# Projections of a hybrid decoder step: the sample rows' column-group steps in pairs behind every second place

## The chip, the cores and the metric

One core of one Trainium2 chip runs the whole kernel. The metric is the device time of one execution in microseconds (us), from its runs the median.

## The reference, cut to what matters

The reference is one inference step of two decoder layers for a prompt group (1024 rows) and a sample group (8 sequences of 4 new rows, 32 rows together) that share the same weights. Three things in it are large matrix products of rows with a weight matrix, and the change is in these alone:

```
layer 0:  h0 = rmsnorm(x) @ even_w_in      rows x 1024 by 1024 x 3584
          x1 = x + (mix0 * silu(z)) @ even_w_out      1024 x 1024
layer 1:  h1 = rmsnorm(x1) @ odd_w_in                 1024 x 2864
          x2 = x1 + (mix1 * silu(z)) @ odd_w_out      1024 x 1024
          y  = rmsnorm(x2)
```

Between them stand the attention and retention parts of the two layers. Each product is wanted for the 1024 prompt rows and for the 32 sample rows. The change alters no value that is computed and no sum's order.

## The kernel before, in words

**Tiling of the prompt rows.** The contraction of 1024 is cut into KD = 8 slices of 128. The prompt rows are NT = 8 tiles of 128 rows. The weight columns are cut into chunks that fit one accumulator bank of 512 columns: 7 chunks of 512 in the first projection, 3 chunks of 342 or 340 for an output projection, 6 chunks of 478 (the last 474) for the second input projection. One row tile against one column chunk is called a *place* here, and places are numbered through a projection (chunk times 8 plus tile). A place is 24 matmuls into one bank: for each slice three products of split operands (`y_lo` with `w_hi`, `y_hi` with `w_lo`, `y_hi` with `w_hi`). These are L489 (`h_acc`) in `project` and L1115 (`x_acc`) in `project_out`. The three banks `acc` rotate. VectorE copies a finished one out (L436, L1004), SyncE stores it (L313, L718).

**The sample rows.** 32 rows would leave three quarters of the array's columns idle. So the sample rows take another form: their transposed rows `yT_s` (128 x 32) are the stationary operand, in plain fp32, and a group of 4 x 448 weight columns (4 x 256 in an output projection, 4 x 358 in the second input projection) streams as four slices that go to four groups of 32 rows of one bank, `acc_s`. For one slice of the contraction that is one *side step*: four matmul calls, which the profile shows as 8 instructions (L501 in `project`, L1129 in `project_out`), each with a weight load of 32 columns. Eight side steps finish one column group. There are 2 groups (16 steps) in the first projection, 1 + 2 groups (24 steps) in the first `project_out`, 1 group (8 steps) in the second.

**The order of the work.** It is written out by hand, for each engine in its own block. A table `step_at` says behind which place which side step stands, and the same table is read by three engines:

- TensorE, behind the products of a place (L516 to L518, L1149 to L1151): `side_step(s)` waits for its weights (`side_in`), at the first step of a later group also for the evacuation of the one before, then issues its matmuls. The last counts up `side_used`.
- SyncE, behind the store of that place (L348 to L353, L805 to L810): `load_side(s + 2)` waits until step s has been done, then loads the weights of step s + 2 into one of two buffers `w_side` (WS = 2). Behind the last step of a group it stores the 32 rows (`store_side`).
- VectorE, behind the copy of that place, only at the last step of a group (`take_side`, L442 or L1013, L1015).

In the first projection one side step stands behind every third place from 8 on (8, 11, ... 53 of 0 to 55). In the first `project_out` they stand behind every second: 8, 10, ... 22 for the output columns, 32, 34, ... 62 for the next projection's (the places go to 71). In the second they stand behind each of 8 to 15 (of 0 to 23). Behind places 18 to 23 of the first `project_out` (`last_out`) and some after it TensorE also turns rows of the next operand (`turn`, L1100), behind the side step where there is one. At the start of chunk 4 of the first `project_out` SyncE also issues the loads of the compressor's weights (`load_compressor`, L748 to L760), ahead of that chunk's stores and side loads.

The lines that matter:

```
step_at = {NT + pace * s: s for s in range(n_steps)}                     # L235, pace = 3
step_at = {NT + (2 if norm_to is None else 1) * s: s for s in range(KD)} # L550
step_at[(first_next + 1) * NT + (n_next - 1) * NT // (n_steps - KD) * (s - KD)] = s
```

Of the kernel before, what the change touches and what calls it, by code (L numbers as in the profile page):

```python
# [223 lines left out]
def project(nc, constants, src, w, n_cols, dst, gain, pair):  # L224
# [7 lines left out]
    n_sides = n_cols // side_chunks  # L232
    n_steps = n_sides * KD
    pace = (NT * (n_chunks - 1)) // n_steps
    step_at = {NT + pace * s: s for s in range(n_steps)}  # L235
    name = dst[0].tensor.name

    def cols_of(i):
# [5 lines left out]
    with Phase(nc) as ctx:  # L244
# [39 lines left out]
        with nc.Block() as block:  # L284
            @block.sync
            def _(sp):
                def load_rows(t, n):
                    b = t % 2
                    if t >= 2:
                        sp.wait_ge(turned[b], t // 2)  # L290
                    sp.dma_start(x[0:n, b, :], src[0][t * P:t * P + n, :] if t < NT else src[1]).then_inc(loaded[b], 16)

                def load_first(j):
                    fr = w[KP * j * P:KP * (j + 1) * P, cols_of(0)].rearrange("(k p) c -> p k c", p=P)
                    sp.dma_start(w_raw[:, KP * j:KP * (j + 1), 0:width(0)], fr).then_inc(first_in[j], 16)

                def load_w(i):
                    if i == 1:
                        sp.wait_ge(first_cut, FIRST_PARTS)
                    else:  # L300
                        sp.wait_ge(w_cut, i - 1)
                    sp.dma_start(w_raw[:, :, 0:width(i)], w[:, cols_of(i)].rearrange("(k p) c -> p k c", p=P)).then_inc(w_in, 16)

                def load_side(s):
                    q, k = divmod(s, KD)
                    if s >= WS:
                        sp.wait_ge(side_used, s - WS + 1)
                    sp.dma_start(w_side[s % WS][:, :], w[k * P:(k + 1) * P, q * side_chunks:(q + 1) * side_chunks]).then_inc(side_in[s % WS], 16)

                def store(i, t):  # L310
                    b, u = out_buffer(i, t)
                    sp.wait_ge(evacuated[b], u + 1)
                    sp.dma_start(dst[0][t * P:(t + 1) * P, cols_of(i)], outb[:, b, 0:width(i)]).then_inc(stored[b], 16)  # L313

                def store_side(q):
                    sp.wait_ge(side_evacuated, q + 1)
                    for j in range(SIDE):
                        c0 = q * side_chunks + j * side_chunk
                        sp.dma_start(dst[1][:, c0:c0 + side_chunk], out_s[j * NS:(j + 1) * NS, :]).then_inc(side_stored, 16)

                load_rows(0, P)
                constants.load(sp, ident_in)
                sp.dma_start(g[:, :], gain.partition_broadcast(P)).then_inc(gain_in, 16)
                load_first(0)
                load_rows(1, P)
                for j in range(1, FIRST_PARTS):
                    load_first(j)
                for t, n in tiles[2:]:
                    load_rows(t, n)
                    if t == 4:  # L330
                        load_w(1)
                    if t >= 3:
                        store(0, t - 3)
                for s in range(WS):
                    load_side(s)
                for t in range(NT - 2, NT):
                    store(0, t)
                for i in range(1, n_chunks):
                    if i + 1 < n_chunks:
                        load_w(i + 1)  # L340
                    for t in range(NT):
                        store(i, t)
                        if i == n_chunks - 1 and t == 1:
                            n_needed = -(-pair.last_column // chunk) * NT
                            for b in range(3):
                                sp.wait_ge(stored[b], 16 * ((n_needed - b + 2) // 3))
                            pair.load(sp)
                        s = step_at.get(i * NT + t)  # L348
                        if s is not None:
                            if s + WS < n_steps:  # L350
                                load_side(s + WS)
                            if s % KD == KD - 1:
                                store_side(s // KD)  # L353
                for b in range(3):
                    pair.landing.counts[b] = 16 * ((n_chunks * NT - b + 2) // 3)
                sp.wait_ge(side_stored, 16 * SIDE * n_sides)
# [45 lines left out]
            def _(dve):  # L402
# [35 lines left out]
                def take_side(q):  # L438
                    dve.wait_ge(side_used, KD * (q + 1))
                    if q:  # L440
                        dve.wait_ge(side_stored, q * 16 * SIDE)
                    nc.vector.tensor_copy(out_s[:, :], acc_s[:, 0:side_chunk]).then_inc(side_evacuated, 1)  # L442
# [18 lines left out]
                for i in range(1, n_chunks):  # L461
                    for t in range(NT):
                        take_product(i, t)
                        if t == CUT_AFTER and i + 1 < n_chunks:
                            w_low_part(i + 1)
                        s = step_at.get(i * NT + t)
                        if s is not None and s % KD == KD - 1:
                            take_side(s // KD)

            @block.tensor  # L470
            def _(pe):
# [40 lines left out]
                for i in range(1, n_chunks):  # L512
                    pe.wait_ge(w_cut, i)
                    for t in range(NT):
                        products(i, t)
                        s = step_at.get(i * NT + t)  # L516
                        if s is not None:
                            side_step(s)  # L518


def project_out(nc, ident, src, w, dst, gates, residual, gain, following=None, norm_to=None, early=None, quad=None, first=None):
# [25 lines left out]
            sides.append(("next", q, side_next))  # L547
    side_width = max(x[2] for x in sides)
    n_steps = KD * len(sides)
    step_at = {NT + (2 if norm_to is None else 1) * s: s for s in range(KD)}  # L550
    for s in range(KD, n_steps):
        step_at[(first_next + 1) * NT + (n_next - 1) * NT // (n_steps - KD) * (s - KD)] = s
    name = dst[0].tensor.name
    order = tuple(range(NT)) if early is None else early.order

# [3 lines left out]
    with Phase(nc) as ctx:  # L559
# [56 lines left out]
        def number(p, t):  # L616
            return p * NT + t
# [57 lines left out]
        with nc.Block() as block:  # L675
            @block.sync
            def _(sp):
# [101 lines left out]
                for p in range(1, n_passes):  # L779
# [18 lines left out]
                    for t in range(NT):  # L798
                        if p != last_out:
                            store(p, t)  # L800
                            if comp is not None and p == n_passes - 2 and t < 4:
                                comp.load_table(sp, t)
                        elif norm_to is None:
                            store_completed(t)
                        s = step_at.get(number(p, t))  # L805
                        if s is not None:
                            if s + WS < n_steps:
                                load_side(s + WS)
                            if s % KD == KD - 1:
                                store_side(s // KD)  # L810
                        if p == last_out and norm_to is not None and t:
                            store_normed(t - 1, P)
                        if p == last_out and norm_to is not None and t == 5:
                            sp.wait_ge(sample_ready, 1)
                            sp.dma_start(norm_to[1], x[0:NS, 1, :]).then_inc(sample_stored, 16)
                        if p == last_out and len(held) <= t < NT - 2:
                            load_kept(t + 2)
# [117 lines left out]
            def _(dve):  # L935
# [70 lines left out]
                def take_side(q):  # L1006
                    what, qq, width = sides[q]
                    dve.wait_ge(side_used, KD * (q + 1))
                    if q:
                        dve.wait_ge(side_stored, q * 16 * SIDE)  # L1010
                    if what == "out":
                        dve.wait_ge(side_res_in, 16 * SIDE)
                        nc.vector.tensor_tensor(out_s[:, 0:width], acc_s[:, 0:width], res_s[:, :], ALU.add).then_inc(side_evacuated, 1)  # L1013
                    else:
                        nc.vector.tensor_copy(out_s[:, 0:width], acc_s[:, 0:width]).then_inc(side_evacuated, 1)  # L1015
# [38 lines left out]
                for p in range(1, n_passes):  # L1054
                    for t in range(NT):
                        take_product(p, t)
                        s = step_at.get(number(p, t))
                        if s is not None and s % KD == KD - 1:
                            take_side(s // KD)
                        if p == last_out:  # L1060
                            if t:
                                norm_rows(t - 1, P)
# [29 lines left out]
            def _(pe):  # L1092
# [50 lines left out]
                for p in range(1, n_passes):  # L1143
                    pe.wait_ge(w_cut, p)
                    for t in range(NT):
                        if p == first_next:
                            y_ready(t, True)
                        products(p, t)
                        s = step_at.get(number(p, t))  # L1149
                        if s is not None:  # L1150
                            side_step(s)  # L1151
                        if p == last_out and norm_to is None and t >= 2:
                            turn(t - 2, P, True)
# [2354 lines left out]
```

## Time and profile before

| | |
|---|---|
| median of 3 runs | 1883.34 us (1883.16 to 1883.73) |
| the profiled execution | 1882.95 us |
| its span, first to last instruction | 1881.2 us |
| mean granted TensorE clock | 0.981 |
| TensorE matmuls busy | 1806.8 us (96%) |
| VectorE, ScalarE, GpSimd busy | 889.9, 704.5, 402.6 us |
| first projection | about 15 to 346 us of the span |
| first output projection with the second input projection | about 600 to 985 us |
| last output projection | about 1768 to 1877 us |

The span leaves out 1.75 us around the first and the last instruction. Matmuls overlap in the pipeline, so a row's duration is longer than the distance to the next one; distances between starts say what an instruction costs in a stream.

### The profile page before, as it was taken

To read this page: it belongs to the slowest core of one execution; us is meant where nothing else is said; L and a number is where in the kernel's file an instruction comes from. 1 tells how busy PE (TensorE), PEld (TensorE's weight loads), DVE (VectorE), ACT (ScalarE), POOL (GpSimd) and SP (SyncE) were. 2 spreads that over 40 slices of the span, in tenths; PEclk is the share of its full clock that TensorE was granted. 3 is DMA by queue.
4 is the path that set the end of the run, shared out by engine and by line. 5 is a ranking of instruction groups with operands and counts; after the bars stand their busy time and mean duration, and the time that the engine had idled before them with its cause. 6 is when DMAs were issued, how large, how long until landed. Compare 5 with 4: busy or idle time off the path is not lost. (4 is left out here: it accounts for less than half of the span.)

```text
span 1881.2 us, 35705 instructions
## 1 busy us (share of the span) xinstructions
PE 1806.8 (96%) x13758; PEld 1496.2 (80%) x13758; DVE 889.9 (47%) x2638; ACT 704.5 (37%) x1541; POOL 402.6 (21%) x576
## 2 busy tenths in 40 slices
PE   7999999999898999999999999999799999999898
PEld 6777777688876998878888787787588888888887
DVE  5322222587556444222413323333778778777534
ACT  5100000375333232000003323233677777777423
POOL 0000000000661000000005221221366565565100
PEclk9999999999897999999998999999899999999999
DMA  6444434554879663744425332434400000000564
GB/s 214 157 142 148 152 130 129 195 162 129 271 232 309 220 227 112 224 146 157 131 71 183 133 116 87 158 124 137 130 19 24 25 24 12 20 14 13 194 192 139
DMA packets 158606, 254.11 MB, mean 135 GB/s; under 512 B 33867, under 2 KB 109896, under 8 KB 154088
## 3 DMA queue, kind: packets, MB, share of 16 engines
q1 hardware_dynamic: 143976, 206.02, 34.1%
q0 software_dynamic: 4608, 33.56, 4.8%
q10 hardware_dynamic: 9856, 12.26, 2.2%
q8 instruction: 112, 1.84, 0.4%
q14 instruction: 54, 0.44, 0.1%
HBM read 205.88 MB, written 52.96 MB: 138 GB/s over the span
## 5 line engine op out<-in xcount | busy, mean ns | idle before, releaser
L1841 POOL TENSOR_SCALAR sparse_pr<-sparse_pr,sparse_coef,sparse_gate 128x63 f32<-128x63 f32 (+8 forms) x384 | 245.6, 659 | 176.5 <-DVE sparse_coef L1791 176.5
L1115 PE MATMUL x_acc<-x_w_hi,x_y_lo 128*128 128x478 f32 (+3 forms) x768 | 275.1, 358 | 2.7 <-DVE x_y_lo L963 2.6
L1115 PE MATMUL x_acc<-x_w_lo,x_y_hi 128*128 128x478 f32 (+3 forms) x768 | 269.6, 351 | 0.0
L1115 PE MATMUL x_acc<-x_w_hi,x_y_hi 128*128 128x478 f32 (+3 forms) x768 | 269.2, 351 | 0.0
L1730 ACT ACTIVATE sparse_pr<-sparse_pr,sparse_nmax 128x63 f32<-128x63 f32 (+8 forms) x384 | 227.6, 595 | 74.9 <-DVE sparse_nmax L1785 74.8
L489 PE MATMUL h_acc<-h_w_hi,h_y_lo 128*128 128x512 f32 x448 | 178.0, 397 | 0.8 <-DVE h_y_lo L414 0.8
L489 PE MATMUL h_acc<-h_w_lo,h_y_hi 128*128 128x512 f32 x448 | 175.2, 391 | 0.0
L489 PE MATMUL h_acc<-h_w_hi,h_y_hi 128*128 128x512 f32 x448 | 175.2, 391 | 0.0
L1115 PEld LDWEIGHTS x_acc<-x_w_hi,x_y_lo 128*128 128x128 f32 x768 | 145.9, 190 | 29.4 <-issue 14.7
L1115 PEld LDWEIGHTS x_acc<-x_w_hi,x_y_hi 128*128 128x128 f32 x768 | 145.8, 190 | 11.3
L1115 PEld LDWEIGHTS x_acc<-x_w_lo,x_y_hi 128*128 128x128 f32 x768 | 146.1, 190 | 10.4
L436 DVE COPY cmp_w<-h_acc 128x512 f32<-128x512 f32 x56 | 38.7, 691 | 244.4 <-PE h_acc L489 244.4
L1653 PE MATMUL sparse_ps<-cmp_lent,sparse_qT 64*128 64x384 f32 (+3 forms) x928 | 138.6, 427 | 5.7 <-DVE sparse_part L1785 5.3
L1665 PE MATMUL sparse_ps<-constants_shared,sparse_pr 128*128 128x128 f32 x1120 | 129.9, 274 | 2.2 <-ACT sparse_prT L1548 1.4
L1691 PE MATMUL sparse_ps_o<-sparse_prT,ss_pieces 128*64 128x128 f32 x2112 | 128.3, 273 | 0.0
L1665 PEld LDWEIGHTS sparse_ps<-constants_shared,sparse_pr 128*128 128x128 f32 x1120 | 122.1, 141 | 6.8 <-issue 2.9
L1785 DVE CUSTOM_DVE_ANT_0 sparse_pr<-sparse_ps,cmp_w 128x63 f32<-128x63 f32 (+4 forms) x384 | 120.9, 370 | 10.2 <-PE sparse_ps L1653 10.2
L1550 DVE COPY sparse_prT<-sparse_ps 128x384 f32<-128x384 f32 (+1 forms) x152 | 94.0, 621 | 65.3 <-PE sparse_ps L1665 61.6
L1004 DVE COPY x_out<-x_acc 128x478 f32<-128x478 f32 (+1 forms) x48 | 31.4, 655 | 192.4 <-PE x_acc L1115 181.0
L1691 PEld LDWEIGHTS sparse_ps_o<-sparse_prT,ss_pieces 128*64 128x64 f32 x2112 | 116.9, 137 | 3.1 <-issue 2.7
L2891 DVE TENSOR_TENSOR ss_x_lo<-ss_ps_t,ss_x_hi 128x512 fp32r<-128x512 f32 x64 | 44.2, 691 | 153.4 <-ACT ss_x_hi L2885 153.4
L3041 PE MATMUL ss_ps_h<-ss_x_lo,ss_w_hi 128*128 128x512 f32 x256 | 111.0, 434 | 1.7 <-ACT ss_hid L3187 1.7
(397 smaller groups left out, 3063.3 us busy)
## 6 DMA issues: line engine op xcount, KB each, us to landing
h<-cmp_w SPq DMA_DIRECT2D x56, 256.0 KB, 2.1
h_w_side<-in_even_w_in SPq DMA_DIRECT2D x16, 896.0 KB, 5.2
h_w_raw<-in_even_w_in SPq DMA_DIRECT2D x6, 2048.0 KB, 8.3
x_w_side<-in_odd_w_in SPq DMA_DIRECT2D x16, 716.0 KB, 4.9
cmp_lent<-in_odd_w_in SPq DMA_DIRECT2D x5, 1912.0 KB, 9.4
h<-x_out SPq DMA_DIRECT2D x40, 239.0 KB, 2.4
ev_unit<-in_cache_a_k SPq DMA_DIRECT2D x4, 2048.0 KB, 10.0
ev_unit<-in_cache_a_v SPq DMA_DIRECT2D x4, 2048.0 KB, 11.4
```

The costliest lines, as they stand in the source:

```text
L436: nc.vector.tensor_copy(outb[:, b, 0:width(i)], acc[b][:, 0:width(i)]).then_inc(evacuated[b], 1)
L489: last = nc.tensor.matmul(acc[b][:, 0:width(i)], rows[:, k, t * P:(t + 1) * P], weights(cols, i)[:, k, :], start=(k == 0 and a == 0), stop ...
L1115: last = nc.tensor.matmul(acc[b][:, 0:passes[p][3]], left[:, k, t * P:(t + 1) * P], weights(right, p)[:, k, :], start=(k == 0 and a == 0), ...
L1550: ins = nc.vector.tensor_scalar(to, src, -SCALE, None, ALU.mult) if negated else nc.vector.tensor_copy(to, src)
L1653: ins = nc.tensor.matmul(to[e][:, o:o + b - a], qT[i % 2][half, t * P:(t + 1) * P], rhs, start=True, stop=True)
L1665: last = nc.tensor.transpose(to[:, x:x + P], pr[:, e, at:at + P], con("ident"))
L1691: ins = nc.tensor.matmul(ps_o[e * HD:(e + 1) * HD, cols], lhs, rhs, start=br == segs[0][0] and k == s0, stop=br == segs[-1][0] and k + P > ...
L1730: nc.scalar.activation(row, row, ACT.Exp, scale=-1.0, bias=nmax[u % UB][:, e * NBR + br:e * NBR + br + 1], accum_out=lsum[u % UB][:, e * N ...
L1785: nc.vector.tensor_tensor_reduce(out=row_of(e, a, b, blocks), in0=bank("score", (c, e))[:, o:o + b - a], in1=bias, scale=1.0, scalar=so_fa ...
L1841: nc.gpsimd.tensor_scalar(row, row, one, gate[:, t, 2 * i + e, (br + 1) % 3:(br + 1) % 3 + 1], ALU.mult, ALU.mult).then_inc(scaled, 1)
L2891: nc.vector.tensor_tensor(x_lo[n % N_X][:, 0:XW], ps_t[nb][:, :], x_hi[n % N_X][:, 0:XW].bitcast(F32), ALU.subtract).then_inc(bank_free[nb ...
L3041: ins = nc.tensor.matmul(ps_h[c][:, :], w[m][:, lw, c * P:(c + 1) * P], x[b][:, s:s + XW], start=l == 0 and s == 0 and i == 0, stop=l == K ...
```

## The change

The table holds, for each place, a tuple of steps in place of one step. Steps 2j and 2j + 1 both stand behind the place at which step 2j + 1 alone stood; behind the place of step 2j there is none. The three engines' blocks go over the tuple.

```
-    step_at = {NT + pace * s: s for s in range(n_steps)}
+    steps_at = {NT + pace * (s + 1): (s, s + 1) for s in range(0, n_steps, 2)}
...
-                        s = step_at.get(i * NT + t)
-                        if s is not None:
+                        for s in steps_at.get(i * NT + t, ()):
                             if s + WS < n_steps:
                                 load_side(s + WS)
                             if s % KD == KD - 1:
...
-                        s = step_at.get(i * NT + t)
-                        if s is not None and s % KD == KD - 1:
-                            take_side(s // KD)
+                        for s in steps_at.get(i * NT + t, ()):
+                            if s % KD == KD - 1:
+                                take_side(s // KD)
...
-                        s = step_at.get(i * NT + t)
-                        if s is not None:
+                        for s in steps_at.get(i * NT + t, ()):
                             side_step(s)
...
-    step_at = {NT + (2 if norm_to is None else 1) * s: s for s in range(KD)}
-    for s in range(KD, n_steps):
-        step_at[(first_next + 1) * NT + (n_next - 1) * NT // (n_steps - KD) * (s - KD)] = s
+    steps_at = {NT + (2 if norm_to is None else 1) * (s + 1): (s, s + 1) for s in range(0, KD, 2)}
+    for s in range(KD, n_steps, 2):
+        steps_at[(first_next + 1) * NT + (n_next - 1) * NT // (n_steps - KD) * (s + 1 - KD)] = (s, s + 1)
```

The three uses in `project_out` change in the same way as those in `project`. The pairs then stand behind places 11, 17, ... 53 of the first projection (8 pairs), behind 10, 14, 18, 22 and 34, 38, ... 62 of the first `project_out` (4 and 8 pairs), and behind 9, 11, 13, 15 of the second (4 pairs). The weight buffers, the matmuls, the copies and the stores are the same in number and size.

## Rows read from the trace of the kernel before

**Rows 1.** Busy time by stretch; the columns stand in the first line.
```profile
core 0: us, PE busy (x) PEld busy (x) DVE busy (x) ACT busy (x) POOL busy (x), PEclk, DMA share, GB/s
...
63.00:345.00 282.00, 282.00 (x1295) 220.05 (x1294) 56.03 (x55) 18.14 (x5) 0.00 (x0) 1.00 0.40 138
345.00:600.00 255.00, 235.45 (x2554) 184.80 (x2552) 166.52 (x580) 123.98 (x272) 69.65 (x101) 0.94 0.69 219
```
**Rows 2.** Waits in the first projection, 70 to 340 us: total, times, longest.
```profile
DVE cmp_w L436 <- PE h_acc L489: 213.0, 46, 5.9
...
PEld h_acc L489 <- issue: 11.7, 16, 0.7
```
**Rows 3.** Timeline of TensorE, first projection: start, duration, line, tiles, shape, count.
```profile
107.89 0.96 PE L501 MATMUL h_acc_s<-h_w_side,h_yT_s 128*32 128x448 f32 x8
108.78 0.50 PE L489 MATMUL h_acc<-h_w_hi,h_y_lo 128*128 128x512 f32 x1
...
114.36 0.39 PE L489 MATMUL h_acc<-h_w_hi,h_y_lo 128*128 128x512 f32 x1
...
119.80 0.39 PE L489 MATMUL h_acc<-h_w_hi,h_y_lo 128*128 128x512 f32 x1
...
126.22 0.50 PE L489 MATMUL h_acc<-h_w_hi,h_y_lo 128*128 128x512 f32 x1
```
**Rows 4.** The same, second input projection: starts of places 30, 31, 48 and 50.
```profile
749.99 0.38 PE L1115 MATMUL x_acc<-x_w_hi,x_y_lo 128*128 128x478 f32 x1
...
755.20 0.38 PE L1115 MATMUL x_acc<-x_w_hi,x_y_lo 128*128 128x478 f32 x1
...
851.79 0.37 PE L1115 MATMUL x_acc<-x_w_hi,x_y_lo 128*128 128x478 f32 x1
...
863.15 0.38 PE L1115 MATMUL x_acc<-x_w_hi,x_y_lo 128*128 128x478 f32 x1
```
**Rows 5.** The same, output projections: half a step, a whole; places 8 to 10.
```profile
652.38 0.42 PE L1129 MATMUL x_acc_s<-x_w_side,x_yT_s 128*32 128x256 f32 x4
652.38 0.64 PE L1129 MATMUL x_acc_s<-x_w_side,x_yT_s 128*32 128x256 f32 x8
...
1806.92 0.32 PE L1115 MATMUL x_acc<-x_w_hi,x_y_lo 128*128 128x342 f32 x1
...
1810.54 0.31 PE L1115 MATMUL x_acc<-x_w_hi,x_y_hi 128*128 128x342 f32 x1
...
1811.35 0.42 PE L1115 MATMUL x_acc<-x_w_hi,x_y_lo 128*128 128x342 f32 x1
...
1815.90 0.42 PE L1115 MATMUL x_acc<-x_w_hi,x_y_lo 128*128 128x342 f32 x1
```
**Rows 6.** The same, a burst of such steps elsewhere: its first 8, 12, 16 instructions.
```profile
540.84 0.61 PE L2268 MATMUL ev_ps_o<-ev_v_new,ev_pT 32*32 32x512 f32 x4
541.38 1.06 PE L2274 MATMUL ev_ps_o<-ev_unit,ev_pT 128*32 128x512 f32 x8
541.38 1.50 PE L2274 MATMUL ev_ps_o<-ev_unit,ev_pT 128*32 128x512 f32 x12
541.38 1.92 PE L2274 MATMUL ev_ps_o<-ev_unit,ev_pT 128*32 128x512 f32 x16
543.23 0.30 PE L2224 MATMUL ev_ps_t<-constants_shared,ev_unit 96*128 96x96 f32 x1
```
**Rows 7.** TensorE's wait, 600 to 945 us, for a side load.
```profile
PE x_acc_s L1129 <- DMA x_w_side<-in_odd_w_in: 0.5, 1, 0.5
```
**Rows 8.** Timeline of the weight loads: one side step.
```profile
125.33 0.16 PEld L501 LDWEIGHTS h_acc_s<-h_w_side,h_yT_s 128*32 128x32 f32 x8 [0.35 <-issue]
```
**Rows 9.** DMA issues: 1803 to 1845, one at 678, two at 632 us; KB each, us to landing.
```profile
ss_pieces<-in_odd_w_out SPq DMA_DIRECT2D x6, 512.0 KB, 4.2
x_w_side<-in_even_w_out SPq DMA_DIRECT2D x1, 512.0 KB, 11.5
x_w_side<-in_even_w_out SPq DMA_DIRECT2D x2, 512.0 KB, 7.9
```

More of the change, by code:

```diff
@@ L804, in _ @@
                             store_completed(t)
-                        s = step_at.get(number(p, t))
-                        if s is not None:
+                        for s in steps_at.get(number(p, t), ()):
                             if s + WS < n_steps:
@@ L1056, in _ @@
                         take_product(p, t)
-                        s = step_at.get(number(p, t))
-                        if s is not None and s % KD == KD - 1:
-                            take_side(s // KD)
+                        for s in steps_at.get(number(p, t), ()):
+                            if s % KD == KD - 1:
+                                take_side(s // KD)
                         if p == last_out:
@@ L1148, in _ @@
                         products(p, t)
-                        s = step_at.get(number(p, t))
-                        if s is not None:
+                        for s in steps_at.get(number(p, t), ()):
                             side_step(s)
```

## The prediction

> **What bounds the kernel now.** I read the busy time by stretch first. Between 63 and 345 us, in the first projection, TensorE is busy for 282.00 of 282 us at a granted clock of 1.00, and VectorE, ScalarE and the DMA engines are far from full [rows 1]. The waits agree: VectorE waits 213 us in that stretch for TensorE's products, while TensorE's weight loads have 16 short idle times of at most 0.7 us with no releaser but "issue" [rows 2]. Sixteen is the number of side steps. So TensorE sets the time here, and a stream that is whole except around the side steps is what the reader is to see. The other two projections look the same; only the places differ.
>
> **What one side step costs now.** I read the timeline of TensorE and go by starts, because durations overlap. In the first projection place 15 starts at 108.78, place 16 at 114.36, 17 at 119.80, and 18, with a side step ahead of it, at 126.22 [rows 3]. The undisturbed place takes 119.80 - 114.36 = 5.44 us; three of them would take 16.32; with one side step they take 126.22 - 108.78 = 17.44. A side step costs 1.12 us. In the second input projection an undisturbed place takes 755.20 - 749.99 = 5.21, and two with one side step take 863.15 - 851.79 = 11.36 [rows 4]: 0.94 us. In the last output projection the 23 distances from 1806.92 to 1810.54 give 0.157 us each, so 3.78 for 24, and a place with a side step takes 1815.90 - 1811.35 = 4.55 [rows 5]: 0.77 us.
>
> **What the same step costs inside a burst.** The two slices-of-four of a step are what its work consists of. The trace has such work back to back: in the retention part 16 instructions of 512 columns follow each other, and the burst grows from 1.06 over 1.50 to 1.92 us with each four more [rows 6]. That is 0.43 us for four slices of 512 columns, and eight to twelve crosses from one step (with its own weights) to the next. By columns: 448 take 0.376, 358 take 0.30, 256 take 0.215. The side step itself agrees, with 0.42 and 0.64 for four and eight instructions of 256 columns [rows 5]. A whole step in a burst then costs 0.75, 0.60 and 0.43 us. What is over in the single step (0.37, 0.34, 0.34 us) is the change of form: from products to side step and back. It does not seem to depend on the burst's length: behind the single step the next matmul starts 0.07 us before the burst ends (107.89 + 0.96 = 108.85, against 108.78 [rows 3]), behind the burst of 16 also (541.38 + 1.92 = 543.30, against 543.23 [rows 6]).
>
> **The change, part by part.** It removes no matmul, copy or transfer. It removes 24 of 48 bursts: 8 in the first projection, 4 + 8 in the first `project_out`, 4 in the second.
> - First projection: 8 x 0.37 = 3.0 us.
> - Second input projection: 8 x 0.34 = 2.7 us.
> - The two output projections: 8 x 0.34 = 2.7 us. One of these eight stands ahead of transposes instead of products; I keep the same figure.
> - One wait for a side load, 0.5 us, in the second input projection [rows 7]. It is step 10 behind place 36, whose load was issued late behind the compressor's big weight loads. Now it stands behind place 38, some 11 us later. I count 0.4 as gained.
>
> Sum: 8.8 us. What is added is one boundary inside each of 24 pairs. Its price isn't in this kernel in the same form. From below it is nothing, as at the boundary between steps in [rows 6] (and below nothing isn't possible, as the columns must stream). From above it is the boundary from L2268 to L2274, where the stationary rows go from 32 to 128 and a wait for a load stands: 541.38 - 540.84 = 0.54 us in place of 0.43, so 0.11 us more, and 24 of them are 2.6 us. I take nothing, since the burst inside L2274 has the side step's own form.
>
> Here a rule speaks against the change. The second four weight loads of a side step are done within 0.16 us of its first matmul, while all matmuls ahead of them still run on the same 128 rows [rows 8]: the trace shows weight loads that overlap matmuls of the same rows. The Trainium skill (TensorE: Matmul & The Clock Gate, Part 3, "What overlaps and what doesn't") says that a weight load overlaps matmuls in flight only when its row group differs. By that rule the second step's weights would be loaded in the open, and the saving would be that of the second rival below; by the row it is whole.
>
> **What hides the rest.** On SyncE the loads of steps s + 2 and s + 3 are now issued together behind the pair. The time from issue to need stays two pair-distances' worth of places: six places in the first projection, four in the first `project_out`, two in the last. Only the last is short: two places of 3.78 us and the 0.34 around them leave about 7.9 us for two loads of 512 KB. One alone lands in 4.2 us; two with another of 512 KB beside them took 7.9 as a median [rows 9]. There is nothing else large in that stretch, so I cost it at nothing, with a thin cover. SyncE's queue: behind the pair it holds the load issues for one step longer (0.75 us), and the next store isn't due until the next place ends 5 us later. VectorE's queue: `take_side` waits behind the same place as before, 0.4 to 0.75 us longer; three accumulator banks cover that. The last step of each group keeps its place, so nothing after a projection starts later. No transfer of the later stages is started ahead of a barrier by a clock of its own, so a gain should carry through.
>
> **Rivals.**
> - *Open weight loads at the inner boundary.* Each of 24 boundaries costs 0.11 us and slows the first slice of the next step by 0.02, as ahead of L2274. The saving falls by 3.1 to 5.7 us: 1877.6. For it: those rows. Against it: [rows 8] and the even growth in [rows 6].
> - *The gain is taken back by a DMA-fed stage.* Between 345 and 600 us the DMA engines are busy for 0.69 of the time and TensorE isn't full [rows 1]. If that stage ends with its transfers and those don't start earlier, the first projection's 3.0 us are lost: 1877.5. Against it: the stage's loads are issued behind the projection's end.
> - *Late side loads in the last projection; the slower case.* The mechanism: three pairs (steps 2 to 7) wait for the second load of the two. It decides when a load takes more than about 7.9 us. The worst of this size took 11.5 us, beside a larger weight load [rows 9]. Then each pair waits 3.6 us, 10.8 in all, against 8.8 gained: 2.0 us slower, 1885.3. It would need that traffic, which isn't there at 1803 to 1845 us.
> - *The step's cost lies in the steps and not in the change of form.* Then two in a row cost twice the single price and nothing moves: 1883.3. Against it stands the whole of [rows 6].
>
> **How the numbers follow.** The profiled execution took 1882.95 us, 1.75 over its span and 0.4 under the median; the sum made against it gives 1874.2, and against the median of the runs 1883.34 - 8.8 = 1874.5. Chances: forecast 0.74, open weight loads 0.12, taken back 0.07, late loads 0.03, no effect 0.04. From above the range takes in both partial cases (1877.6) and a little more; from below 1.5 us for differences in size. 1873.0 to 1878.5 leaves out the last two cases and some error of size. A measurement of this kernel can tell about 0.2%, 3.8 us, from no change. The forecast and both partial cases lie beyond it (0.93); no effect, and most of the late loads, within it (0.05); worse late loads beyond it on the other side (0.02).
>
> **What the changed profile would show.** In the first projection every burst of L501 has 16 instructions, about 0.96 + 0.75 = 1.71 us long, with 8 bursts, and six places take 6 x 5.44 + 1.12 + 0.75 = 34.5 us (now 34.9). TensorE's idle "issue" times ahead of L489 halve to 8. If the inner distance between the second and third four instructions is 0.51 in place of 0.38 us, the first rival is right. A wait of L1129 for `ss_pieces` loads would show the third. The wait in [rows 7] is gone. If the three projections are shorter by 3.0, 4.5 and 1.3 us and the whole isn't, the second rival holds.

## The result

The changed kernel takes 1873.32 us as the median of 5 runs (1871.92 to 1874.43), the kernel before beside it 1883.16. The ratio is 0.9944 (95% interval 0.9933 to 0.9955), which is 10.5 us less; the two medians differ by 9.8. The forecast was 8.8 us less: 1874.5 in a range of 1873.0 to 1878.5. The direction and the mechanism hold; the saving was put too low. The median itself lies inside the range, but 0.9944 of the 1883.34 us from which the prediction starts is 1872.8, just below the range's lower end. The profiled execution took 1872.26 us, its span 1870.5.

Busy time by stretch in the changed kernel, columns as in [rows 1]. The second line reaches from the start of place 8 to that of place 55 of the first projection, the third from place 23 to 26 of the first `project_out`:

```profile
core 0: us, PE busy (x) PEld busy (x) DVE busy (x) ACT busy (x) POOL busy (x), PEclk, DMA share, GB/s
...
66.68:337.61 270.93, 270.93 (x1257) 214.42 (x1256) 55.31 (x54) 18.13 (x5) 0.00 (x0) 1.00 0.40 142
...
701.58:721.28 19.70, 16.99 (x99) 15.21 (x98) 13.07 (x15) 5.99 (x10) 0.00 (x0) 1.00 0.62 214
```

The same two stretches of the kernel before:

```profile
67.48:341.08 273.60, 273.60 (x1257) 213.12 (x1256) 55.34 (x54) 18.14 (x5) 0.00 (x0) 1.00 0.41 140
...
706.58:728.26 21.69, 18.54 (x99) 16.41 (x98) 13.17 (x15) 6.43 (x10) 0.00 (x0) 0.92 0.56 180
```

In the first both kernels keep TensorE busy throughout at the full clock, with the same 1257 matmuls, and the changed one is 2.67 us shorter. In the second the granted clocks differ (0.92 and 1.00). No row of the change explains that, and I come back to it.

The burst itself, answering to [rows 3]: the first in the first projection, by its first 4, 8, 12 and all 16 instructions (from four stretches of TensorE's timeline).

```profile
88.53 0.58 PE L500 MATMUL h_acc_s<-h_w_side,h_yT_s 128*32 128x448 f32 x4
88.53 0.96 PE L500 MATMUL h_acc_s<-h_w_side,h_yT_s 128*32 128x448 f32 x8
88.53 1.33 PE L500 MATMUL h_acc_s<-h_w_side,h_yT_s 128*32 128x448 f32 x12
88.53 1.71 PE L500 MATMUL h_acc_s<-h_w_side,h_yT_s 128*32 128x448 f32 x16
90.17 0.50 PE L488 MATMUL h_acc<-h_w_hi,h_y_lo 128*128 128x512 f32 x1
```

Each four instructions add 0.38 us, and the step from 8 to 12, which crosses from one side step to the next, is no dearer (0.37). The weight loads of the same burst, first those of the first step, then those for the first half of the second:

```profile
88.53 0.16 PEld L500 LDWEIGHTS h_acc_s<-h_w_side,h_yT_s 128*32 128x32 f32 x8 [0.35 <-issue]
88.93 0.13 PEld L500 LDWEIGHTS h_acc_s<-h_w_side,h_yT_s 128*32 128x32 f32 x4 [0.25 <-issue]
```

The second group is done at 89.06, while the first eight matmuls run until 89.49 (88.53 + 0.96). The waits answer to [rows 2]; they are taken from 63 to 340 us here and from 70 there, which changes VectorE's total, but takes in all side steps in both:

```profile
DVE cmp_w L435 <- PE h_acc L488: 219.5, 48, 6.7
...
PEld h_acc_s L500 <- issue: 6.8, 24, 0.4
PEld h_acc L488 <- issue: 5.9, 8, 0.7
```

The idle times of the weight loads ahead of L489 (now L488) went from 16 with 11.7 us to 8 with 5.9, with the number of bursts. Those ahead of the side steps went from 16 with 5.6 us to 24 with 6.8: the added ones lie inside the bursts, under running matmuls. In the last output projection (columns as in [rows 5]) the burst is there too, with no wait in front of it:

```profile
1801.47 0.32 PE L1112 MATMUL x_acc<-x_w_hi,x_y_lo 128*128 128x342 f32 x1
...
1805.32 1.07 PE L1126 MATMUL x_acc_s<-ss_pieces,x_yT_s 128*32 128x256 f32 x16
1806.32 0.42 PE L1112 MATMUL x_acc<-x_w_hi,x_y_lo 128*128 128x342 f32 x1
...
1810.19 0.32 PE L1112 MATMUL x_acc<-x_w_hi,x_y_lo 128*128 128x342 f32 x1
```

### The profile page after: what moved, and what is told of

Read it like the earlier page. It is cut to its first block and busy times, and to the rows that moved or that the text cites. A ratio compares the mean times of both kernels' runs of the same rounds, so it can differ in the third digit from the quotient of the medians.

```text
span 1870.5 us, 35705 instructions
## 1 busy us (share of the span) xinstructions
PE 1796.5 (96%) x13758; PEld 1497.9 (80%) x13758; DVE 888.6 (48%) x2638; ACT 704.4 (38%) x1541; POOL 401.5 (21%) x576
## 5 line engine op out<-in xcount | busy, mean ns | idle before, releaser
L488 PE MATMUL h_acc<-h_w_hi,h_y_lo 128*128 128x512 f32 x448 | 176.7, 394 | 0.8 <-DVE h_y_lo L413 0.8
L488 PE MATMUL h_acc<-h_w_lo,h_y_hi 128*128 128x512 f32 x448 | 175.0, 391 | 0.0
L488 PE MATMUL h_acc<-h_w_hi,h_y_hi 128*128 128x512 f32 x448 | 174.8, 390 | 0.0
L1781 DVE CUSTOM_DVE_ANT_0 sparse_pr<-sparse_ps,cmp_w 128x63 f32<-128x63 f32 (+4 forms) x384 | 120.8, 369 | 11.7 <-PE sparse_ps L1649 11.7
```

The source lines that it names most:

```text
L488: last = nc.tensor.matmul(acc[b][:, 0:width(i)], rows[:, k, t * P:(t + 1) * P], weights(cols, i)[:, k, :], start=(k == 0 and a == 0), stop ...
L1781: nc.vector.tensor_tensor_reduce(out=row_of(e, a, b, blocks), in0=bank("score", (c, e))[:, o:o + b - a], in1=bias, scale=1.0, scalar=so_fa ...
```

## The experiments

The experiments edit the tables, and f_proj the weight buffers too. The edits are shown against the changed kernel. "Single" below means the old table with one step in each tuple. For every profiled execution I worked out the distance between the starts of the first matmul of certain places, from the timelines; this is the table to which the experiments refer (us; P1 is the first projection, P2 the first `project_out`, P3 the second):

```
stretch            before c_before e_shift e_first e_next  e_out   after c_after f_proj e_late
P1 place 8 to 55   273.60  273.60  273.60  270.93  273.60 273.60  270.93  270.93 269.15 270.93
P2 place 8 to 22    61.04   61.04   61.04   61.03   61.03  59.27   59.27   59.27  59.27  59.27
P2 place 22 to 26   27.00   27.01   25.46   27.00   27.00  26.97   25.43   27.04  26.89  26.73
P2 place 26 to 64  214.38  214.42  213.84  214.43  211.12 214.24  211.12  211.12 211.13 211.12
P3 place 8 to 16    36.25   36.25   36.25   36.25   36.25  34.78   34.78   34.78  34.78  47.61
all other time    1268.88 1268.64 1269.69 1267.23 1269.27 1267.90 1268.93 1270.25 1266.01 1271.33
```

The four executions that the table leaves out:

```
stretch          e_first2  e_hide c_after2 f_proj2
P1 place 8 to 55   270.93  273.60   270.93  269.15
P2 place 8 to 22    61.03   59.97    59.27   59.27
P2 place 22 to 26   28.05   27.03    25.44   27.01
P2 place 26 to 64  214.96  214.84   211.12  211.13
P3 place 8 to 16    36.25   36.25    34.78   34.78
all other time    1271.18 1267.61  1268.95 1270.69
```

Where TensorE is never kept waiting a stretch repeats within 0.05 us. "All other time" (the span less the five rows) varies by some 5 us from execution to execution, and not with the edit (e_late's holds 1.7 us of its own, behind place 16). P2 places 8 to 22 hold seven single steps, but only six joined ones, since step 6 has moved behind place 22; for the output columns only the sum with the next row, places 8 to 26, compares like with like.

**c_before and c_after: both kernels once more.**

> The kernel before, once more, for a second trace of it. Theory A (the change saves 8.7 us by its 24 removed bursts, and what the two profiled executions differ by beyond that is where the granted clock happened to fall): time 1883 us within 1.5; the stretches from place 8 to 55 of the first projection (273.60 us) and from place 26 to 64 of the first project_out (214.4 us) repeat within 0.1 us, while the stretches between them, where TensorE waits, differ from the first trace by 0.3 to 1.5 us. Theory B (the rest is systematic, from the change): those in-between stretches repeat within 0.2 us too, place 24 taking 7.6 us as in the first trace.

> The changed kernel, once more. Theory A: 1873.5 to 1874.5 us against 1883.2, and place 24 of the first project_out takes either 6.1 or about 7.6 us, with the clock granted there. Theory B: 1872.3 to 1873, place 24 takes 6.1 us again, and every stretch repeats.

Measured: 1884.2 us (ratio 0.9999, 0.9990 to 1.0008), and 1874.07 us (0.9944, 0.9931 to 0.9958). Place 22 to 26 takes 27.04 us in this execution of the changed kernel, against 25.43 in the first, with the fall of the granted clock back. So the 1.6 us there in the first pair of profiles do not come with the change each time. Two details were expected otherwise: in the kernel before this stretch did repeat (27.01 for 27.00), as Theory B had it, and place 24 took 6.9 us in the changed one, neither 6.1 nor 7.6. In "all other time" the first pair happens to agree (1268.88 and 1268.93). The median lies where Theory A put it (1873.5 to 1874.5), but the ratio stays at 0.9944, which is more than its 8.7 us.

**e_first: pairs in the first projection alone**, twice, the second time as e_first2.

```
-    steps_at = {NT + (2 if norm_to is None else 1) * (s + 1): (s, s + 1) for s in range(0, KD, 2)}
-    for s in range(KD, n_steps, 2):
-        steps_at[... (s + 1 - KD)] = (s, s + 1)
+    (single)
```

> Pairs in the first projection alone. Theory A: 8 bursts fewer at 0.33 us (three-place distance and after-effect as in the changed kernel's trace), 2.7 us less than before; the stretch from place 8 to 55 takes 270.93 us and the other projections' side steps cost what they did. Theory B (a part of the gain is made elsewhere by shifting): 3.5 us or more less.

> Pairs in the first projection alone, once more. Theory A (2.67 us by TensorE's own stream, the first comparison's 4.5 us were the spread of the executions): 0.9985, with an interval that holds 0.9986. Theory B (something beyond the projection gains 1.5 to 2 us by it): 0.9975 again.

Measured: 1878.75 us (0.9976, 0.9967 to 0.9985), then 1880.83 us (0.9984, 0.9975 to 0.9993). The stretch is 270.93 us as in the changed kernel, 2.67 less, or 0.33 per removed burst. That ratio is 0.9986; the second interval holds it and the first just misses it. The second span, 1882.4 us, was even longer than the one of before, with the same 270.93 us in it. So the spread can explain most of the first figure; whether it explains all of it stays open.

**e_next: pairs for the next projection's columns alone.**

```
-    steps_at = {NT + pace * (s + 1): (s, s + 1) for s in range(0, n_steps, 2)}
-    steps_at = {NT + (2 if norm_to is None else 1) * (s + 1): (s, s + 1) for s in range(0, KD, 2)}
+    (single)
```

> Pairs for the next projection's columns alone (places 34 to 62 of the first project_out). Theory A: 8 bursts fewer at 0.34 and the wait of 0.5 us for a side load gone, 3.3 us less than before; places 26 to 64 take 211.1 us. If the wait comes back in another place: 2.7 us.

Measured: 1880.02 us (0.9983, 0.9974 to 0.9992), 3.2 us less, and 211.12 us from place 26 to 64: 3.3 less, as expected. The wait of [rows 7] is gone, and gone in every kernel whose table has these pairs. Where it stands it took 0.3 to 1.0 us (0.5 in three profiles, 0.3 in e_out, 0.9 in e_hide, 1.0 in e_first2).

**e_out: pairs for the output columns alone.**

```
-    steps_at = {NT + pace * (s + 1): (s, s + 1) for s in range(0, n_steps, 2)}
-    for s in range(KD, n_steps, 2):
-        steps_at[... (s + 1 - KD)] = (s, s + 1)
+    (single)
```

> Pairs for the output columns alone (4 pairs in the first project_out, 4 in the last). 8 bursts fewer at 0.34: 2.7 us less than before. If the pair's second load came late in the last projection there would be a wait of TensorE for it and less saved.

Measured: 1879.91 us (0.9983, 0.9974 to 0.9992), 3.2 us less. In P3 the four pairs save 1.47 us (36.25 to 34.78), 0.37 each, without a wait for a load. In P2 the four save 61.04 + 27.00 - 59.27 - 26.97 = 1.80 us, 0.45 each: more than one removed burst is worth.

**e_shift: even steps one place later, no pairs.**

```
-    steps_at = {NT + pace * (s + 1): (s, s + 1) for s in range(0, n_steps, 2)}
+    steps_at = {NT + pace * s + (s + 1) % 2: (s,) for s in range(n_steps)}
```

and likewise in the first `project_out`.

> No pairs: 48 bursts as before, but every even step stands one place later in the first projection and the first project_out (the last is unchanged). Theory A (only the number of bursts counts): 1883 us as before, within 1 us, the steps' price 1.12 and 0.94 us each. Theory B (where the steps stand is what pays): some of the 9.8 us comes without pairs, 1 us or more less.

Measured: 1882.69 us (0.9998, 0.9989 to 1.0007). The projection stretches are as before (273.60, 61.04, 36.25), save the 0.5 us of the side load's wait, which is gone here too (213.84). Moving a step gains nothing but that wait; changing the form less often does.

**e_hide: two pairs only**, steps 0 and 1 behind place 10 and steps 6 and 7 behind place 22 of P2; all else single. The part of the edit that makes the pairs:

```
-    steps_at = {NT + (2 if norm_to is None else 1) * (s + 1): (s, s + 1) for s in range(0, KD, 2)}
+    steps_at = {NT + (2 if norm_to is None else 1) * s: (s,) for s in range(KD)}
+    if norm_to is None:
+        for s in (0, 6):
+            del steps_at[NT + 2 * s]
+            steps_at[NT + 2 * (s + 1)] = (s, s + 1)
```

> The kernel before, with only two pairs: steps 0 and 1 behind place 10, steps 6 and 7 behind place 22 of the first project_out; all else single. Theory A: the pair at place 22 saves more than the change of form, since its second step now runs in the time in which TensorE waits for the next turned rows anyway (2.7 us in the changed kernel, 3.15 before): 0.34 for the first pair and 0.72 to 0.8 for the second. From place 8 to 26 the stretch is then shorter by 1.1 us than before (88.04 us, or 86.5 where the clock stays whole there). Theory B: both pairs save 0.34, and the 0.44 us that the changed kernel gained beyond that come from elsewhere: 0.7 us shorter.

Measured: 1881.13 us in the one execution that there is, too few to compare whole times; its stretches can be read. Place 8 to 22 takes 59.97 us and 22 to 26 takes 27.03, together 87.00 for 88.04. That is 1.04 us for two pairs, where two removed bursts at 0.34 make 0.7. The timeline says why. Before, behind place 22, one side step, the turn, VectorE's cut of the next chunk's weights, and ahead of the next turn an idle time of TensorE that VectorE ends (in brackets):

```profile
705.16 0.64 PE L1129 MATMUL x_acc_s<-x_w_side,x_yT_s 128*32 128x256 f32 x8
...
705.73 1.09 PE L1100 MATMUL x_tps<-constants_shared,cmp_w 128*128 128x128 f32 x8
...
707.33 4.14 DVE L980 TENSOR_TENSOR x_w_lo<-cmp_lent,x_w_hi 128x3824 fp32r<-128x3824 f32 x1 [2.06 <-ACT x_w_hi L877]
...
713.67 1.09 PE L1100 MATMUL x_tps<-constants_shared,cmp_w 128*128 128x128 f32 x8 [3.15 <-DVE cmp_w L949]
```

With the pair behind place 22 (e_hide):

```profile
700.48 1.07 PE L1130 MATMUL x_acc_s<-x_w_side,x_yT_s 128*32 128x256 f32 x16
701.48 1.09 PE L1101 MATMUL x_tps<-constants_shared,cmp_w 128*128 128x128 f32 x8
...
708.99 1.59 PE L1101 MATMUL x_tps<-constants_shared,cmp_w 128*128 128x128 f32 x8 [2.70 <-DVE cmp_w L950]
```

The idle time shrinks from 3.15 to 2.70 us, by about the second step's 0.43. TensorE waits there for rows that VectorE normalizes (L949) behind its cut (L980). That chain doesn't move with the side step: from the start of place 22 (701.27 before, 696.59 in e_hide) the cut starts after 6.06 us and the wait ends after 12.40 us in both. A side step put ahead of that wait runs in it and adds nothing that these traces show.

**f_proj: bursts of four in the first projection**, pairs elsewhere, twice, the second time as f_proj2. The two further weight buffers lie in `x` and `z`, which nobody uses behind place 8.

```
-    SIDE, WS = 4, 2
+    SIDE, WS = 4, 4
-    steps_at = {NT + pace * (s + 1): (s, s + 1) for s in range(0, n_steps, 2)}
+    steps_at = {NT + pace * (s + 3): tuple(range(s, s + 4)) for s in range(0, n_steps, 4)}
-        w_side = [sb(f"w_side{b}", [P, side_chunks]) for b in range(WS)]
+        w_side = [sb(f"w_side{b}", [P, side_chunks]) for b in range(2)]
+        w_side += [a[:, :, :].rearrange("p b c -> p (b c)")[:, 0:side_chunks] for a in (x, z)]
...
+                    if s == 2:
+                        sp.wait_ge(turned[NT % 2], NT // 2 + 1)
```

> The changed kernel, with bursts of four steps in the first projection (behind places 17, 29, 41, 53): the third and fourth weight buffer lie in memory that the rows and their squares have left by then. If each removed burst saves the same, 4 more at 0.33 to 0.37: 1.4 us less than the changed kernel, and a burst costs 1.12 + 3 x 0.752 = 3.4 us or up to 0.1 more for its after-effect. If a longer burst has a dearer exit (the changed kernel's is 0.035 us dearer than the single one): 1.1 us less or so.

> Bursts of four in the first projection, pairs elsewhere, once more beside the changed kernel itself. Its stream says 1.78 us less than the changed kernel (the stretch from place 8 to 55 took 269.15 for 270.93 us): 1871.9 if the changed kernel takes 1873.7. If it takes 1870.3 again, something else gains as well.

Measured: 1870.31 us (0.9931, 0.9917 to 0.9944), then 1871.22 (0.9934, 0.9921 to 0.9947), with the changed kernel at 1872.32 in the same comparison. The stretch takes 269.15 us: 1.78 less than with pairs, 0.44 per removed burst, above both figures that were expected. Its place 8 to 55 are 47 places of 5.44 us, 255.68; what is over is 13.47 us for 4 bursts of four, 3.37 each, 15.25 for 8 pairs, 1.91 each, and 17.92 for 16 singles, 1.12 each. Less 0.752 per step, the changes of form cost 0.36, 0.40 and 0.37. The difference lies in the exit: the place with the burst ahead of it grows by 0.75 us with each further step (6.42, 7.17 and, for two more, 8.68 us), while the place after that takes 5.57 us behind four, 5.61 behind a pair and 5.58 behind a single. Why isn't known. This is the fastest version measured, 13.0 and 12.2 us under the kernel before by the medians.

**c_after2: the changed kernel, beside those.**

> The changed kernel, once more, on the chip of these others: 1873.7, and its stretches of the projections repeat within 0.1 us (270.93, 211.12, 34.78).

Measured: 1872.32 us (0.9943, 0.9931 to 0.9956); the stretches repeat (270.93, 211.12, 34.78), and place 22 to 26 takes 25.44 us, again without the fall of the clock.

**e_late: the third rival made to happen**, in the last projection.

```
-    steps_at = {NT + (2 if norm_to is None else 1) * (s + 1): (s, s + 1) for s in range(0, KD, 2)}
+    group = 2 if norm_to is None else 4
+    steps_at = {NT + (2 if norm_to is None else 1) * (s + group - 1): tuple(range(s, s + group)) for s in range(0, KD, group)}
```

> The changed kernel, but with bursts of four steps on two weight buffers in the last projection, so that steps 3 and 4 of each burst wait for loads that are only issued when steps 1 and 2 are done: the third rival's mechanism, made to happen. Issue lag 0.7 us and 4.2 to 5 us to landing less one step, twice, against 2 bursts fewer: 8 to 10 us slower than the changed kernel, more (up to 3 us) if the granted clock falls to half after the idle time.

Measured: 1885.89 us (1.0014, 1.0005 to 1.0024), slower than the kernel before, and by the ratios 13 us above the changed kernel: the upper end of what was expected, with the fall of the clock. The profiled execution is the slowest of the ten (1888.79 us). First the waits of TensorE between 1790 and 1850 us; then its timeline, the first burst, whose third and fourth steps come late:

```profile
PE x_acc_s L1127 <- DMA ss_pieces<-in_odd_w_out: 9.1, 3, 4.2
```
```profile
1814.87 1.07 PE L1127 MATMUL x_acc_s<-ss_pieces,x_yT_s 128*32 128x256 f32 x16
1819.61 0.64 PE L1127 MATMUL x_acc_s<-ss_pieces,x_yT_s 128*32 128x256 f32 x8 [3.68 <-DMA ss_pieces<-in_odd_w_out]
1821.41 1.08 PE L1127 MATMUL x_acc_s<-ss_pieces,x_yT_s 128*32 128x256 f32 x8 [1.16 <-DMA ss_pieces<-in_odd_w_out]
```

and the busy time by stretch around it:

```profile
1799.70:1816.00 16.30, 16.24 (x114) 15.37 (x112) 2.58 (x5) 2.47 (x1) 0.00 (x0) 1.00 0.21 63
1816.00:1832.00 16.00, 11.23 (x63) 9.94 (x64) 0.51 (x1) 0.00 (x0) 0.00 (x0) 0.79 0.48 153
1832.00:1847.40 15.40, 11.02 (x84) 8.47 (x82) 4.44 (x4) 0.00 (x0) 0.00 (x0) 0.90 0.32 103
```

The waits are 9.1 us; the granted clock falls from 1.00 to 0.79 and 0.90 behind them, that is from 2.4 GHz to its lower level of 1.2 GHz for a part of the time, and the slower matmuls are the rest. The last step lasts 1.08 us in place of 0.64. From place 8 to 16 the projection is 12.8 us longer, although it has two bursts (0.7 us) fewer, and place 16, at the lower clock, takes 1.7 us more: for 9.1 us of waits this execution pays about 15.

## Why the prediction was right or wrong

- **A burst costs a change of form, nearly whatever its length: right.** Apart from the wait of [rows 7], the stretches without waits shrink where and only where bursts are removed, and e_shift, which moves steps without joining them, keeps all 48 and their cost. It isn't the steps' own wait for their weights either: each step of a pair has one, and the boundary inside the pair costs nothing. Side steps differ from products in two ways, though, by the 32 columns of their stationary operand and by plain fp32 in place of fp32r, and no run tells which of them costs the time.
- **Nothing at the inner boundary: right.** 0.37 us from the eighth to the twelfth instruction, where the upper bound was 0.11 more. The second step's weights are loaded while the first runs (until 89.06 of 89.49). The rule that was weighed against the change, of the Trainium skill (TensorE: Matmul & The Clock Gate, Part 3, "What overlaps and what doesn't"), is that a weight load overlaps a matmul only in another row group. It doesn't hold in this trace: both steps use all 128 rows. The rival of the open weight loads falls. (Its upper figure, 5.7 us, has no working in the prediction: 24 x 0.13 is the 3.1.)
- **First projection 3.0 us: mis-sized.** It is 2.67. The single step was taken at 1.12 and the second of a pair at 0.75, which is right; but the pair's exit costs 0.035 us more than the single's. I had argued that the two are equal from the first matmul behind one burst of each kind alone. The places after it show the difference (5.61 us, 5.58 before).
- **Second input projection 2.7 and 0.4 us: right**, 3.3 measured (0.34 each, and 0.5 of wait; against e_shift, which has no wait, 2.7).
- **Output projections 2.7 us: the step that failed.** They gain 3.27 (1.80 and 1.47). In the last, a burst is worth 0.37 in place of 0.34, mostly because an undisturbed place takes 3.76 us (places 9 and 10 of e_late) and not the 3.78 of the prediction. In the first the pair behind place 22 hides its second step: "I keep the same figure" for the step ahead of the transposes left out that TensorE waits 3.15 us behind it anyway. That wait was in the trace and I did not ask which steps stand ahead of it. In e_hide the ordinary pair takes 0.36 of the 1.04 us, and 0.7 are left for this one.
- **The sum.** 2.67 + 1.80 + 3.27 + 1.47 = 9.2 us by TensorE's own stream, against 8.8. That these are so near is in part luck: the first projection was put 0.3 too high, which hides some of the 0.6 missing from the output projections. With the failed step mended the forecast would be 1874.1, inside the range, so this step alone doesn't carry the result past its end. The comparisons say 10.5, 10.5 and 10.7 us by the ratios (0.9944, 0.9944, 0.9943), and 9.8, 9.6 and 11.1 by the medians. 9.2 us are a ratio of 0.9951, inside each interval, but all three lie on the same side, and about 1.3 us beyond the stream stays open. One candidate was the granted clock behind the idle time ahead of place 24, whose fall costs 1.6 us there: it stayed whole in 2 of 3 executions of the changed kernel and in neither of the kernel before. Over all fourteen profiles this evens out: it stayed whole in 2 of 8 with the pair behind place 22 and in 1 of 6 (e_shift) with a single step there. A second hint is that the excess shows by the ratios in all seven comparisons whose first projection is joined (0.3 to 2.0 us) and not in e_next and e_out (3.2 us each, where the stream gives 3.3). But "all other time" is 1266.0 to 1271.2 us in the profiles of the first kind and 1267.6 to 1269.7 in the others, so a further gain is neither shown nor excluded.
- **The range: its lower end was too tight.** I gave 1.5 us below the forecast for sizes and nothing for the spread of the executions, which is 1878.5 to 1887.5 us for the kernel before alone. The medians of the changed kernel alone lie at 1873.32, 1874.07 and 1872.32.
- **SyncE's queue and the loads: right.** In the last projection the six loads landed in 4.1 to 6.0 us, where the forecast had about 7.9 between issue and need, and TensorE waited for none. The slower rival's mechanism is real (e_late), but needs the loads issued with no places between.
- **Taken back by a later stage: this rival falls.** "All other time" does not grow with the saving (the figures stand under the sum).

## What to carry to other kernels

When a minor stream of matmuls in another form is woven into a dense one, count the changes of form and not only the columns: each one removed saved 0.33 to 0.44 us here, so join the minor steps as far as buffers allow, but issue their loads at least a transfer's time ahead, as a late load costs its wait and a slower clock behind it. Ask of each piece that can be moved whether it can stand ahead of a wait that is there anyway. Judge such small changes by stretches in which the bound engine never waits; they repeat within 0.05 us where whole executions spread over several.

## What was not expected of the hardware

A burst of 32 instructions leaves the stream 0.04 us cheaper than one of 16, and about as cheaply as one of 8 (the place behind takes 5.57, 5.61 and 5.58 us). And the granted clock falls behind the same 2.70 us of idle time in one execution of the same kernel (c_after) and not in others (the first profile and c_after2); it costs 1.6 us there, and 2.6 in e_first2 behind 3.1 us of idle time.
